# Context tile first in the output stage, matmuls of ones in the last gaps of attention, and the waits of the overflow test inside its chunk

## The chip, the cores and the metric

The kernel runs on one core of a Trainium2 chip. The metric is the time on the device in microseconds, the median over several executions. Before the change the median of three runs is 1055.93 us (1055.47 to 1056.59).

The engines are called PE (TensorE, matmuls), DVE (VectorE), ACT (ScalarE), POOL (GpSimd) and SP (SyncE, which here only issues DMAs). One core has 16 DMA engines.

## What is computed

One layer of a backbone with 512 latent tokens and 128 context tokens, in fp32, D = 1024. Both groups go through the same weights; they differ in the vectors of the adaLN modulation (`g1`, `a2`, `b2` below come from them), in attention and in the scans.

```python
def trunk_layer(x, mod, p, lru_h0, ctx_ckv, ctx_kr):
    sh1, sc1, g1, sh2, sc2, g2 = mod
    h = rmsnorm(x, p['norm1_g']) * (1 + sc1) + sh1
    mix, ctx_state = token_mixing(h, p, lru_h0, ctx_ckv, ctx_kr)
    x = x + g1 * mix
    h = rmsnorm(x, p['norm2_g']) * (1 + sc2) + sh2
    x = x + g2 * hier_moe(h, p)
    return x, ctx_state

# token_mixing ends with
#   o = blocked_attend(q, k, v)                    8 heads
#   gates = sigmoid(h @ w_gate)                    4 branches
#   out = sum(gates * branches) @ w_out

def hier_moe(h, p):
    t = h.reshape(B * L, D)
    g_sel = argmax(t @ w_gr + b_gr)                # 1 of 4 groups
    top_v, top_i = top_k(e_logit of g_sel, 2)      # 2 of its 8 experts
    y = sum over experts of (silu(t @ w1) * (t @ w3) * combine) @ w2   # 32 experts, width 256
```

## The kernel before

It is one program written by hand, engine by engine, with semaphores. Nothing schedules it: the order of each engine's instructions is the order in which the lines of its section stand, and a wait holds all that stands behind it on that engine. The sections are SP (lines 586 to 776), PE (780 to 1409), ACT (1413 to 1711), DVE (1715 to 2429) and POOL (2433 to 2674).

The 640 tokens are `TT` = 5 tiles of 128; tiles 0 to 3 are the latent ones (`LT` = 4) and tile 4 is the context. The stages, by the times of the profiled execution, are:

- **Projections and mixers**, 0 to 270 us. At its start PE runs matmuls of `ones` by `ones` (`spin`, L825) while it waits for weights.
- **Attention**, 270 to 368 us, in 40 units (`UNITS`), each a head and a tile of queries. PE does `scores(i + 2)` and then `probabilities_T(i)` (L1050), which transposes what ACT and DVE made of the scores of unit i. Once in ten units there are the values matmuls (`values`, L1061). The last units are of the context tile, which has one block of keys, so they are short: 5 transposes for a latent unit and one for a context unit.
- **Gates and merge**, 368 to 686.7 us: `h @ w_gate`, the branch products, sums.
- **Output stage**, 686.7 to 790 us. For each tile t and half h of 512 columns: `output(t, h)` (PE, L1172, 8 matmuls with `w_out`, two rows each in the trace), `residual(t, h)` (DVE, L2181 to L2184: times `g1_row`, plus x, times `a2_row`), `x1_T(t, h)` (PE, transposes), sums of squares on ACT, `variance(t)` and `modulated(t)` (DVE: scale and `b2_row`, giving `h2[t]`, which SP stores together with x1), `logits(t, h)` (PE, L1193, 4 matmuls each), `select(t)`, `weights(t)`, `places(t)` and `first(t)` (DVE, the choice of experts and the slot of every token), `counts_ahead`, `prefix` and `table` (PE, small matmuls on it). After the last tile PE runs `first_rows` (L1219, 16 rows for each tile), from which the table of tokens for every expert slot comes; GpSimd gathers rows of h2 by that table (L2615).
- **Experts**, 790 to 1050 us, in 17 units (`UNITS_E`, u = 0 to `LAST` = 16), two experts each but for one. The weights of an expert, 3 MB, go through a ring of six buffers `wexp`, parts of r_a, r_c, r_w, r_ys, r_bv and r_h; SP loads the next w1/w3 (`load_w13`) when `hidden` of the unit in the buffer is done (`s_A`), the next w2 (`load_w2`) when `project` is done (`s_Y`). PE: `pair_T` (L1309), `hidden` (L1316), `hidden_T` (L1323), `project` (L1332). Results are scattered by GpSimd (L2619). An expert has 64 slots; tokens that don't fit go to overflow chunks, and a test between the units 14 and 15 reads their number `n_x` into a register of each engine. With these inputs it is 1, which means that no chunk is run.

The rows `g1_row`, `a2_row` and `b2_row` hold one set for all tiles in the output stage, each 1024 values on 128 partitions. They stand for the latent tiles first and are loaded anew, from `rows_scratch`, for tile 4:

```python
            load_row("xres", g1_row, 0)
            load("xres", x1, x_dram)
            load_row("xres", a2_row, 2)
            load_row("xres", b2_row, 4)
...
                if t == LT - 1:
                    sp.wait_ge(s_x1, 2 * LT)
                    load_row("xres", g1_row, 1)
                sp.wait_ge(s_h2, t + 1)
                if t == LT - 1:
                    load_row("xres", a2_row, 3)
                    load_row("xres", b2_row, 5)
```

so `g1_row` is asked for when `residual(3, 1)` has read it, a2 and b2 when `modulated(3)` has, and `residual(4, 0)` waits for all three.

## Time and profile before

| | us |
|---|---|
| median of 3 runs | 1055.93 |
| profiled execution, its own time | 1059.88 |
| its span | 1058.0 |

| stretch | length | PE busy | DVE busy | clock of PE | DMA share |
|---|---|---|---|---|---|
| projections, 0 to 270 | 270.0 | 260.58 | 138.25 | 0.99 | 0.41 |
| attention, 270 to 368 | 98.0 | 90.01 | 49.30 | 0.98 | 0.08 |
| gates, 368 to 686.7 | 318.7 | 318.70 | 190.35 | 1.00 | 0.27 |
| output, 686.7 to 790 | 103.3 | 100.13 | 61.56 | 0.97 | 0.55 |
| experts, 790 to 1040 | 250.0 | 215.77 | 69.42 | 0.94 | 1.00 |
| end, 1040 to 1058 | 18.0 | 7.88 | 6.58 | 0.82 | 0.32 |

The clock is the granted clock of TensorE as a share of full speed (2.4 GHz); the lower level, 1.2 GHz, is 0.50. The DMA share is the mean busy share of the 16 DMA engines. Over the whole span PE is busy for 993.1 us (94%), DVE for 515.5, POOL for 264.8 and ACT for 232.9. The rows of a timeline give the start, the busy time of a group of like instructions, and in brackets the idle time before it with what ended it. A matmul in fp32 stands as two rows.

### The profile page before, as it was taken

How to read it: one execution, taken by the hardware profiler on the slowest of the kernel's cores; microseconds unless marked ns; L12 is line 12 of the kernel's file. 1: busy time of each engine (PE TensorE's matmuls, PEld its weight loads, DVE VectorE, ACT ScalarE, POOL GpSimd, SP SyncE). 2: the span in 40 equal slices, each digit the busy share in tenths (PEclk: the TensorE clock that was granted, in tenths of full speed). 3: DMA queues.
4: the chain of work that ended last, by engine and by line, in shares of the span. 5: the costliest groups of instructions: out<-in, count | busy, mean ns of one | idle time of the engine just before them, and what ended most of it. 6: DMA issues, size and time to landing. Idle time of an engine off the chain costs nothing.

```text
span 1058.0 us, 11696 instructions
## 1 busy us (share of the span) xinstructions
PE 993.1 (94%) x4304; PEld 590.0 (56%) x4304; DVE 515.5 (49%) x1016; ACT 232.9 (22%) x464; POOL 264.8 (25%) x268
## 2 busy tenths in 40 slices
PE   8999999999899999999999999999989997878776
PEld 6666666655555477777777777645574332322221
DVE  3378652246645345567677555538573331322222
ACT  3223330134555311111111111112111111101011
POOL 0333310011630233445364334100010211110101
PEclk9999999999999999999999999999989998998998
DMA  9745356000000271221312311263489999999994
GB/s 369 300 139 222 120 194 234 1 6 2 1 1 1 100 288 50 80 70 50 100 50 86 143 60 61 80 258 120 159 291 381 335 405 399 400 427 397 403 410 130
DMA packets 37609, 193.65 MB, mean 183 GB/s; under 512 B 7642, under 2 KB 12442, under 8 KB 27696
## 3 DMA queue, kind: packets, MB, share of 16 engines
q1 hardware_dynamic: 32784, 182.31, 44.6%
q0 software_dynamic: 4624, 10.06, 3.9%
q8 instruction: 35, 0.57, 0.2%
q10 hardware_dynamic: 144, 0.52, 0.1%
q14 instruction: 22, 0.18, 0.0%
HBM read 185.50 MB, written 14.09 MB: 189 GB/s over the span
## 4 chain that ended last, share of the span: by engine, by line
PE 79%; DMA 10%; DVE 5%; issue 3%; ACT 2%; SPq 1%; POOL 1%; POOLq 0%; DVEq 0%; ACTq 0%
PE psum L1096 23%; PE psum L1316 9%; PE psum L857 8%; PE psum L1130 7%; DMA r_bv<-in_w_e 4%; PE psum L1332 4%; PE psum L950 3%; PE psum L1172 3%; PE psum L1034 3%; DMA r_ys<-rows_scratch 2%; PE psum L1050 2%; PE psum L802 2%; DMA r_w<-in_w_ada 2%; PE psum L1061 2%; PE psum L979 2%
## 5 line engine op out<-in xcount | busy, mean ns | idle before, releaser
L1096 PE MATMUL psum<-r_h,r_w 128*128 128x320 f32 x512 | 143.6, 433 | 0.0
L2591 POOL TENSOR_TENSOR r_w<-r_w 128x512 f32<-128x512 f32 x64 | 84.7, 1330 | 223.0 <-PE psum L1096 155.9
L1096 PEld LDWEIGHTS psum<-r_h,r_w 128*128 128x128 f32 x512 | 97.1, 190 | 40.6 <-issue 0.3
L1096 PE MATMUL psum<-r_ys,r_w 128*128 128x320 f32 x384 | 111.2, 432 | 0.0
L1096 PEld LDWEIGHTS psum<-r_ys,r_w 128*128 128x128 f32 x384 | 73.0, 190 | 30.4
L1601 ACT ACTIVATE r_bv<-r_bv 128x320 f32<-128x320 f32 x64 | 30.1, 470 | 238.8 <-DVE r_bv L2128 238.8
L2619 POOL DMA_INDIRECT out_y<-r_bv,tab x17 | 26.8, 1576 | 204.7 <-DVE r_bv L2392 204.7
L1172 PE MATMUL psum<-r_w,r_bv 128*128 128x512 f32 x160 | 72.2, 597 | 0.0
L2137 DVE TENSOR_TENSOR r_t<-psum,r_t 128x320 f32<-128x320 f32 x112 | 52.2, 483 | 9.3 <-PE psum L1130 8.0
L1675 ACT ACTIVATE r_t<-psum 128x256 f32<-128x256 f32 x17 | 6.5, 384 | 185.6 <-PE psum L1316 183.7
L2114 DVE SCALAR_TENSOR_TENSOR r_t<-r_bv,r_t 128x320 f32<-128x320 f32 x48 | 46.7, 974 | 1.2 <-ACT r_bv L1601 1.2
L2128 DVE TENSOR_TENSOR sqbuf<-psum,r_bv 128x320 f32<-128x320 f32 x32 | 15.7, 492 | 64.4 <-PE psum L1096 64.4
L2372 DVE COPY r_t<-psum 128x256 f32<-128x256 f32 x17 | 7.2, 424 | 81.1 <-PE psum L1323 81.1
L1172 PEld LDWEIGHTS psum<-r_w,r_bv 128*128 128x128 f32 x160 | 29.2, 190 | 30.3 <-issue 30.1
L1316 PE MATMUL psum<-r_c,r_ckv 128*64 128x512 f32 x64 | 31.9, 648 | 7.9 <-issue 7.9
L2072 DVE TENSOR_REDUCE tinys<-psum 128x1 f32<-128x640 f32 (+1 forms) x40 | 28.6, 716 | 18.5 <-PE psum L1035 18.3
L1034 PE MATMUL psum<-r_a,r_bv 96*128 96x512 f32 x64 | 34.5, 620 | 2.5 <-ACT r_bv L1540 0.8
L2128 DVE TENSOR_TENSOR r_bv<-psum,r_bv 128x320 f32<-128x320 f32 x32 | 15.7, 491 | 41.8 <-PE psum L1096 41.8
L2123 DVE TENSOR_TENSOR r_bv<-r_bv,r_t 128x320 f32<-128x320 f32 x48 | 35.8, 745 | 0.4
L2365 DVE SCALAR_TENSOR_TENSOR r_t<-r_t,psum 128x256 f32<-128x256 f32 x17 | 7.2, 421 | 57.9 <-ACT r_t L1675 57.9
L2441 POOL TENSOR_TENSOR tinys<-tinys 128x2 f32<-128x2 f32 (+2 forms) x11 | 7.6, 688 | 108.3 <-DVE tinys L2189 107.8
L1316 PE MATMUL psum<-r_w,lruw 128*64 128x512 f32 x48 | 24.5, 660 | 5.5 <-issue 5.5
(460 smaller groups left out, 2003.9 us busy)
## 6 DMA issues: line engine op xcount, KB each, us to landing
r_a<-in_w_ada SPq DMA_DIRECT2D x8, 2048.0 KB, 7.8
r_w<-in_w_gate SPq DMA_DIRECT2D x32, 512.0 KB, 4.5
r_a<-in_w_e SPq DMA_DIRECT2D x6, 2048.0 KB, 31.9
r_c<-in_w_e SPq DMA_DIRECT2D x5, 2048.0 KB, 31.2
r_c<-in_w_e SPq DMA_DIRECT2D x8, 1024.0 KB, 34.4
r_w<-in_w_e SPq DMA_DIRECT2D x4, 2048.0 KB, 34.3
r_ys<-in_w_e SPq DMA_DIRECT2D x4, 2048.0 KB, 36.5
r_bv<-in_w_e SPq DMA_DIRECT2D x4, 2048.0 KB, 36.6
```

Of the source, the lines that this page charges most:

```text
L857: ins = mm(dst, w_n[:, k, :], z_mix0[:, k // 2, k % 2, :] if n == 4 else x[:, k, :], start=(k == 0), stop=(k == HK - 1))
L950: mm(o[:, 0:512], x, w[:, 0:512], start=(k == 0), stop=(k == KD - 1))
L1034: mm(o[:, 0:NLAT], q, kT[0:QK, h, 0:NLAT], start=True, stop=True)
L1096: ins = mm(gate_bank(u, n), w[:, k, :], x[:, k, :], start=(k == 0), stop=(k == HK - 1))
L1130: ins = mm(branch_bank(u, seq), x_w[:, k, :], xs_[k], start=(k == 0), stop=(k == kb - 1))
L1172: ins = mm(out_bank(t, n), merged[:, k, t * P:(t + 1) * P], w[:, (k % 4) * D + n * 512:(k % 4) * D + (n + 1) * 512], start=(k == 0), stop= ...
L1316: ins = mm(psum[lo:lo + C, slot, 0:2 * FE], xT[:, k, :], w[:, k * 2 * FE:(k + 1) * 2 * FE], start=(k == 0), stop=(k == KD - 1))
L1332: ins = mm(psum[lo:lo + C, slot, n * 512:(n + 1) * 512], hid[:, f, :], w[:, n * 512:(n + 1) * 512], start=(f == 0), stop=(f == 1))
L2114: v.scalar_tensor_tensor(out=merged[:, 2 * i + j, part] if b == 0 else bquad[n], in0=gth[:, j, part], scalar=1.0, in1=bquad[n], op0=ALU.ad ...
L2123: v.tensor_tensor(merged[:, 2 * i + j, part], merged[:, 2 * i + j, part], bquad[n], ALU.add) \
L2137: v.tensor_tensor(bsum[:, dst, :], branch_bank(u, seq), bsum[:, more, :], ALU.add).then_inc(s_badd, 1)
L2591: g.tensor_tensor(w_mix[n], x, y, op).then_inc(s_wm, 1)
```

## The change

1. **The order of the tiles in the output stage.** `TILE = (4, 0, 1, 2, 3)`: step t now works on tile `TILE[t]`, so the context tile is the first. `side(t)` says whether step t is the context (1) or latent (0) and picks the logits' weights and the column of `info`; `tokens_of(t)` gives its rows. The context's g1, a2 and b2 are loaded first, together with the context's x alone (512 KB); behind a wait for all four, the 2 MB of the latent x. g1 of the latent tiles is asked for after `residual(0, 1)`, a2 and b2 after `modulated(0)`. DVE waits for them before `residual(1, 0)`, where it waited before `residual(4, 0)`.
2. **The order within the first tiles** on PE, DVE and ACT is rewritten: PE does `output(2, 0)` whole before `x1_T(1, 0)`, DVE does `modulated(0)` and `select(0)` before `residual(1, 0)`, ACT does `router_exps(0)` earlier.
3. **`load_w13(4)`**, 2 MB into r_bv, is issued by SP behind `load_w2(3)`, no longer behind the waits for the stores of h2 and x1 and for the first transpose of the experts.
4. **Matmuls of ones on PE** before the last three `probabilities_T` (four each, after a wait for the probabilities of the unit before) and before the last `values` (two).
5. **The overflow test.** PE's waits for `s_yd` (the sums of the unit before are drained) and `s_xTd` move into the chunk, and its reading of `n_x` moves to unit 2.

```diff
+TILE = (LT,) + tuple(range(LT))
...
-            load_row("xres", g1_row, 0)
-            load("xres", x1, x_dram)
-            load_row("xres", a2_row, 2)
-            load_row("xres", b2_row, 4)
+            load_row("xres", g1_row, 1)
+            load("xres", x1[:, 0:1, :], x_dram[:, LT:TT, :])
+            load_row("xres", a2_row, 3)
+            load_row("xres", b2_row, 5)
+            sp.wait_ge(loaded["xres"], 64)
+            load("xres", x1[:, 1:TT, :], x_dram[:, 0:LT, :])
...
-                if t == LT - 1:
-                    sp.wait_ge(s_x1, 2 * LT)
-                    load_row("xres", g1_row, 1)
+                if t == 0:
+                    sp.wait_ge(s_x1, 2)
+                    load_row("xres", g1_row, 0)
                 sp.wait_ge(s_h2, t + 1)
-                if t == LT - 1:
-                    load_row("xres", a2_row, 3)
-                    load_row("xres", b2_row, 5)
+                if t == 0:
+                    load_row("xres", a2_row, 2)
+                    load_row("xres", b2_row, 4)
...
             load_w2(3)
+            load_w13(4)
...
             sp.wait_ge(s_xT, 1)
-            load_w13(4)
...
+                if i >= len(UNITS) - 3:
+                    pe.wait_ge(s_prob, i)
+                    spin(4, (i - 1) % 2)
                 probabilities_T(i)
+            spin(2, 0)
             values(H // 2 - 1, 0, TT)
...
             pe.wait_ge(s_x1, 1)
-            output(2, 0, (0, 1))
-            logits(1, 0)
-            output(2, 0, (2, 3, 4, 5))
-            x1_T(1, 1)
-            output(2, 0, (6, 7))
+            output(2, 0, range(KD))
+            x1_T(1, 0)
             pe.wait_ge(s_x1, 2)
             output(2, 1, (0, 1))
+            x1_T(1, 1)
+            logits(1, 0)
+            output(2, 1, (2, 3))
             logits(1, 1)
...
+                if u == 2:
+                    pe.wait_ge(s_slot, 1)
+                    n_x = pe.value_load(xinfo[0:1, XCH:XCH + 1], min_val=1, max_val=XCH)
                 if u != LAST - 2:
                     continue
 
-                pe.wait_ge(s_yd, LAST - 1)
-                pe.wait_ge(s_xTd, LAST + 1)
-                pe.wait_ge(s_slot, 1)
-                n_x = pe.value_load(xinfo[0:1, XCH:XCH + 1], min_val=1, max_val=XCH)
-
                 def chunk(x):
+                    pe.wait_ge(s_yd, LAST - 1)
+                    pe.wait_ge(s_xTd, LAST + 1)
...
-                if t == LT and h == 0:
-                    dve.wait_ge(loaded["xres"], 112)
+                if t == 1 and h == 0:
+                    dve.wait_ge(loaded["xres"], 128)
...
             residual(0, 0)
             residual(0, 1)
-            residual(1, 0)
             variance(0)
             modulated(0)
+            select(0)
+            residual(1, 0)
+            weights(0)
             residual(1, 1)
-            select(0)
             variance(1)
             modulated(1)
-            weights(0)
```

How this moves instructions, first on PE at the end of attention, before the change (L1050 is `probabilities_T`, L1037 `scores` of a context unit, L1061 `values`):

```order
L1050 MATMUL psum<-consts,r_t 128x128 x5
L1037 MATMUL psum<-r_a,r_bv 128x128
L1050 MATMUL psum<-consts,sqbuf 128x128 x5
L1050 MATMUL psum<-consts,r_d 128x128
L1050 MATMUL psum<-consts,r_t 128x128
L1061 MATMUL psum<-r_c,r_bv 64x512 x10
```

and after it, where the same lines are numbered 1060, 1047 and 1071 and L835 is `spin`:

```order
L1060 MATMUL psum<-consts,r_t 128x128 x5
L1047 MATMUL psum<-r_a,r_bv 128x128
L835 MATMUL psum<-ones 128x128 x4
L1060 MATMUL psum<-consts,sqbuf 128x128 x5
L835 MATMUL psum<-ones 128x128 x4
L1060 MATMUL psum<-consts,r_d 128x128
L835 MATMUL psum<-ones 128x128 x4
L1060 MATMUL psum<-consts,r_t 128x128
L835 MATMUL psum<-ones 128x128 x2
L1071 MATMUL psum<-r_c,r_bv 64x512 x10
```

Each of the last three `probabilities_T` and the values now have matmuls of ones ahead of them.

On SP in the output stage, before the change: `rows_scratch` holds the rows, r_h<-in_x is the load of x, r_ys, r_h, r_w and r_bv<-in_w_e are expert weights, h_scratch and out_y the stores of a tile.

```order
L697 DMA r_w<-in_w_out 128x4096 x2
L588 DMA r_ys<-rows_scratch 128x1024
L588 DMA r_h<-in_x 128x5x1024
L588 DMA r_ys<-rows_scratch 128x1024 x2
L670 DMA r_ys<-in_w_e 128x1024
L721 DMA h_scratch<-r_bv 128x1024
```

and after:

```order
L705 DMA r_w<-in_w_out 128x4096 x2
L596 DMA r_ys<-rows_scratch 128x1024
L596 DMA r_h<-in_x 128x1024
L596 DMA r_ys<-rows_scratch 128x1024 x2
L596 DMA r_h<-in_x 128x4x1024
L678 DMA r_ys<-in_w_e 128x1024
L596 DMA r_ys<-rows_scratch 128x1024 x3
L731 DMA h_scratch<-r_bv 128x1024
```

The x3 of the second set of rows stood ahead of the store of tile 3, and stands now ahead of the first store.

On PE in the expert stage, after the change, behind `project` of unit 2 (L1344); L1403 is the reading of `n_x`, which stood, as L1395, behind `project` of unit 14:

```order
L1344 MATMUL psum<-r_bv,r_t 64x512
L1344 MATMUL psum<-r_ys,r_t 64x512
L1403 TENSOR_LOAD xinfo
L1403 ISA x2
L1328 MATMUL psum<-r_w,r_ckv 64x512
```

The reading now stands ahead of the next unit's `hidden` (L1328) early in the stage.

## Rows read from the trace of the kernel before

**Rows 1.** PE timeline, output stage: start, us, instruction [idle before <-releaser].
```profile
686.66 20.76 PE L1172 MATMUL psum<-r_w,r_bv 128*128 128x512 f32 x48
...
758.72 3.60 PE L1172 MATMUL psum<-r_w,r_bv 128*128 128x512 f32 x8
...
763.18 0.39 PE L1204 MATMUL psum<-r_bv,consts 128*128 128x32 f32 x2
...
767.89 1.95 PE L1172 MATMUL psum<-r_w,r_bv 128*128 128x512 f32 x4
771.94 1.08 PE L1193 MATMUL psum<-w_r,r_t 128*128 128x36 f32 x8 [2.09 <-ACT r_t L1630]
...
775.01 1.89 PE L1193 MATMUL psum<-w_r,r_t 128*128 128x36 f32 x8 [0.69 <-ACT r_t L1630]
```

**Rows 2.** Windows: length, PE, PEld, DVE, ACT, POOL busy, PEclk, DMA share, GB/s.
```profile
362.50:365.50 3.00, 3.00 (x8) 0.91 (x10) 0.00 (x0) 0.00 (x0) 0.64 (x1) 0.50 0.97 347
769.80:775.00 5.20, 2.22 (x17) 1.83 (x16) 4.68 (x17) 2.09 (x5) 0.00 (x0) 1.00 0.79 268
775.00:782.00 7.00, 6.99 (x33) 6.99 (x34) 6.24 (x28) 0.59 (x3) 2.30 (x2) 0.51 1.02 400
788.00:790.00 2.00, 2.00 (x20) 1.96 (x19) 0.27 (x3) 0.18 (x1) 0.93 (x1) 1.00 0.06 25
810.00:812.00 2.00, 2.00 (x11) 0.56 (x8) 0.00 (x0) 0.01 (x1) 0.00 (x0) 1.00 0.51 209
850.00:900.00 50.00, 44.53 (x197) 16.37 (x199) 12.58 (x23) 10.11 (x15) 7.80 (x6) 0.90 1.02 403
```

**Rows 3.** PE timeline of the last units of attention.
```profile
351.96 2.79 PE L1061 MATMUL psum<-r_w,r_bv 128*64 128x512 f32 x12
...
359.44 0.74 PE L1050 MATMUL psum<-consts,sqbuf 128*128 128x128 f32 x5 [0.74 <-issue]
...
362.42 6.01 PE L1061 MATMUL psum<-r_c,r_bv 128*64 128x512 f32 x20 [0.37 <-ACT r_c L1591]
```

**Rows 4.** PE timeline at the start of the kernel: matmuls of ones.
```profile
17.74 3.39 PE L825 MATMUL psum<-ones 128*128 128x128 f32 x28
```

**Rows 5.** VectorE timeline at the tail of the output stage.
```profile
764.24 0.69 DVE L2181 TENSOR_TENSOR consts<-psum,r_ys 128x512 f32<-128x512 f32 x1 [6.58 <-DMA r_ys<-rows_scratch]
...
767.98 0.25 DVE L2208 SCALAR_TENSOR_TENSOR r_bv<-psum,tinys,scond 128x36 f32<-128x36 f32 x1
...
772.20 0.68 DVE L2181 TENSOR_TENSOR consts<-psum,r_ys 128x512 f32<-128x512 f32 x1
```

**Rows 6.** Chain of waits from the tail to the first rows: start us, us, what.
```profile
778.17 7.28 PE psum L1219 x48
...
787.84 1.85 PE psum L1219 x16
```

**Rows 7.** Tile r_ys at 757.7, second set of rows: from issue to landing.
```profile
DMA to landing us min/median/max: 4.0/5.1/6.1
```

**Rows 8.** PE timeline of the last two units.
```profile
1031.21 1.08 PE L1316 MATMUL psum<-r_c,r_ckv 128*64 128x512 f32 x1 [2.99 <-issue]
...
1044.93 0.61 PE L1332 MATMUL psum<-r_c,r_t 128*64 128x512 f32 x1 [0.71 <-DVE r_t L2372]
```

**Rows 9.** VectorE timeline, last unit.
```profile
1048.93 0.69 DVE L2392 TENSOR_TENSOR r_bv<-psum,sqbuf 128x512 f32<-128x512 f32 x1
```

**Rows 10.** Tile r_w at 1014.0, last w2 piece: from issue to landing.
```profile
DMA to landing us min/median/max: 28.3/28.3/28.3
```

**Rows 11.** Tile r_w at 790.7, gather of unit 1: from issue to landing.
```profile
DMA to landing us min/median/max: 7.5/7.5/7.5
```

**Rows 12.** Tile r_w at 820.9, a later gather: from issue to landing.
```profile
DMA to landing us min/median/max: 14.7/14.7/14.7
```

**Rows 13.** PE timeline, pair_T of unit 1.
```profile
800.74 1.10 PE L1309 MATMUL psum<-consts,r_w 128*128 128x128 f32 x8
```

**Rows 14.** Tile r_ys at 689.4 to 690.1, first set of rows: from issue to landing.
```profile
DMA to landing us min/median/max: 15.2/16.0/16.7
```

More of the change, by code:

```diff
@@ L567, in wait_quad_free, with side, tokens_of @@
                 eng.wait_ge(s_mdone, 4 * (u - 3 * OUT_PAIRS) + n + 1)
+        def side(t):
+            return 1 if TILE[t] == LT else 0
+        def tokens_of(t):
+            return slice(TILE[t] * P, (TILE[t] + 1) * P)
         def gate_bank(u, n):
@@ L1188, in logits @@
                 pe.wait_ge(s_htd, 2 * t + h + 1)
-                pe.wait_ge(s_wr, 1 if t < LT else 2)
+                pe.wait_ge(s_wr, 1 + side(t))
                 if t >= 2:
@@ L1192, in logits @@
                 for k in range(KD // 2):
-                    ins = mm(psum[:, 2, t % 2 * 512:t % 2 * 512 + LOGITS], xT[h][:, k, :], w_rm[t // LT][h][:, k, :],
+                    ins = mm(psum[:, 2, t % 2 * 512:t % 2 * 512 + LOGITS], xT[h][:, k, :], w_rm[side(t)][h][:, k, :],
                              start=(h == 0 and k == 0), stop=(h == 1 and k == KD // 2 - 1))
@@ L1236, in _ @@
             output(1, 1, (4, 5))
-            x1_T(1, 0)
             logits(0, 1)
@@ L1251, in _ @@
             prefix(0)
-            output(2, 1, (2, 3, 4, 5))
+            output(2, 1, (4, 5, 6, 7))
             x1_T(2, 0)
-            output(2, 1, (6, 7))
             pe.wait_ge(s_x1, 5)
@@ L1643, in _ @@
             take_x1T(0, 1)
+            router_exps(0)
             squares(1, 0)
@@ L2238, in weights @@
                 dve.wait_ge(s_ract, 2 * t + 2)
-                w1, w2 = (info[:, i * TT + t, 1 + t // LT:2 + t // LT] for i in range(2))
+                w1, w2 = (info[:, i * TT + t, 1 + side(t):2 + side(t)] for i in range(2))
                 step(v.tensor_scalar(top(5), top(3), 1.0, top(2), ALU.add, ALU.mult))
```

16 lines of the change are left out of this document (8 added, 8 removed).

## The prediction

> **What bounds the kernel now.** The question for each edit is which wait ends last where it stands, so the stages are read one by one. TensorE is the bound up to about 770 us: the PE timeline of the output stage shows groups of output matmuls back to back from 686.66 on [rows 1]. From 770 to 775 it is busy for 2.22 of 5.20 us, and from 775 to 782 it is busy all the time at a granted clock of 0.51, that is at the lower of its two levels [rows 2]. After that the DMA engines are the bound: between 850 and 900 their share is 1.02, with PE busy 44.53 of 50 us [rows 2]. Between the two there are two holes of the DMA engines, 788 to 790 (share 0.06) and 810 to 812 (share 0.51) [rows 2]. Both are transfers that wait for PE to free a buffer: as PE begins the expert units earlier, the whole DMA-bound stage, and with it the end, comes earlier by as much. So a microsecond saved on PE before 790 is worth a microsecond at the end. The reader is to carry three places from this: the last gaps of attention, the tail of the output stage, and the last unit.
>
> **Part A, constants in the last gaps of attention.** PE waits 0.74 us before the row at 359.44 and 0.37 before the values matmuls at 362.42, with two more such gaps between, and afterwards the clock is at 0.50 (362.5 to 365.5) [rows 2, 3]. The 20 values rows take 6.01 us there. At full clock 12 such rows took 2.79, so 20 would take 4.65: the lower level costs 1.36 [rows 3]. The new matmuls on ones cost 3.39/28 = 0.12 a row, two rows for each matmul, thus 0.97 for a group of four [rows 4]. They start when the wait for the probabilities before is over and end after the gap of 0.74, so they lengthen the path a little where the gap is shorter than 0.97: I take 0.35 in sum, between nothing (all of it in idle time) and 1.0 (one whole group too much). The gates stage behind has no idle time of PE, so what is won stays. A = 1.36 - 0.35 = +1.0; ends +1.36 and, if the clock falls all the same, -1.0.
>
> **Part B, context tile first.** Before, residual(4,0) could not start until the second set of rows (g1, a2, b2 of the context) had landed: VectorE waits 6.58 us and starts at 764.24 [rows 5], though its matmuls were done about half-way through the x8 group of 758.72, near 760.6 [rows 1]. The change loads the second set between tiles 0 and 1. What is late next at the tail is not 3.6 us earlier all along:
> - places(2), behind residual(4,0) on VectorE, needs prefix(2), which stands on PE at 763.18 [rows 1]; it began at about 766.4, behind the residual's three instructions of 0.7 us from 764.24 [rows 5], and can come 2.7 earlier.
> - residual(4,1), at 772.20 [rows 5], needs output(4,1), which ends at 767.89 + 1.95 = 769.84 [rows 1]. It comes 2.3 earlier.
> - so logits(4,1), at 775.01 [rows 1], starts near 772.7, and with counts and table behind it first_rows starts 2.3 earlier than 778.17 [rows 6]; that is the floor of this part.
> Then the clock. The wait of 2.09 us before logits(4,0) [rows 1] shrinks to about 0.4, and the gaps that remain up to 774.3, around logits(4,0) and before logits(4,1) (0.69 now [rows 1]), are near 0.9 and 0.8. If that keeps the higher level, the 48 rows of 7.28 us take three times 1.85, as the 16 rows at 787.84 do: 1.73 less [rows 6]; and logits(4,1), 1.89 for 8 rows against 1.08 at 771.94, takes 0.8 less [rows 1, 6], of which 0.7 lies on the path. Sum 2.3 + 0.7 + 1.73 = 4.75.
> At the head, x comes in two loads and DVE does modulated(0) and select(0) before residual(1,0). a2 and b2 of the latent tiles are asked for when modulated(0) has ended (about 712.0) and, landing as late as the context's did, 6.1 us [rows 7], are there at 718.1 to 718.5. residual(1,0) stands behind select(0); select(3) took from 767.98 to 772.20, 4.2 us [rows 5], and as select(0) starts near 715.1 it ends at 719.3. So the rows are hidden with 0.8 us left. PE meanwhile has output(2,0) whole: 5 halves of 16 rows at 20.76/48 = 0.43 [rows 1] are 34.6, with x1_T(0) and logits(0) (about 2.2) from 686.66, so it is busy until 723.5, and residual(1,0)'s three instructions end near 721.5. I take off 0.3 for one stall of logits(2,0), which is now closer behind its vectors. B = +4.45, ends +2.0 and +4.75. The rest of this part (tokens' numbers, the side of each tile, the w13 piece of r_ys behind a wait that is over near 701) is address work and costs nothing while the DMA engines have room; without this room the piece would be the first of its buffer to be late, but it is used only from 790 on.
>
> **Part C, waits of the overflow test.** Before the last unit PE is idle 2.99 us (row at 1031.21) [rows 8]: it waits for the last sums of the unit before and then loads the register. Without both, hidden(16) starts 2.99 earlier at best, at 1028.2, and since the row at 1031.21 and those behind it go at the lower level (1.08 us), project(16) could come still a little more than 3.0 before 1044.93 [rows 8]. What is late next is the last w2 piece: asked for at 1014.0, landing 28.3 us later, at 1042.3 [rows 10]. So project(16) starts at 1042.4, the last two rows of VectorE (the first at 1048.93 [rows 9]) come 2.5 earlier, and the scatter behind them is unchanged. C = +2.5; ends 0 (the register's load alone costs the gap) and +3.0 (a landing as early as the stage allows). The register's load at unit 2 may cost PE up to the same 2.99; there the DMA engines are the bound with PE idle a tenth of the time [rows 2], so I count 0. If that cover were gone it would cost 1 to 3. Early w13(4): its buffer is free earlier than it is used, and the stage behind is set by the buffers that PE frees, so no gain; the cost is the second rival.
>
> **Sum.** 1.0 + 4.45 + 2.5 = 7.95. The profiled execution takes 1059.88, so 1051.9 for one like it; it lies 3.95 above the median of 1055.93. Applied to the median: 1055.93 - 7.95 = 1047.98, I say 1047.9.
>
> **The rivals.**
> - The clock falls again at the tail of the output stage. Gaps of 0.4, 0.9 and 0.8 within 4 us stand against the one place where I can read it: at 358 to 362, gaps of 0.4 to 0.8 were enough for 0.50 behind them [rows 2, 3]. Then the 1.73 and the 0.7 are not had: 5.5 in sum, 1050.4. For it: that row. Against it: PE has been at full clock with few gaps for long before. 27%.
>  The Trainium skill, "TensorE: Matmul & The Clock Gate", section "What's actually happening", says that the throttled state is the default and that the share of pulses is set by how busy the array has been recently, not by one wait. By that rule three gaps count in sum, as they did at 358 to 362, and the time would be the 1050.4; only if they count singly is it 1047.9.
> - The gather of unit 1 is late. It took 7.5 us to land when it was issued at 790.7 into the empty DMA engines [rows 11], and a later one 14.7 at 820.9 into full ones [rows 12]. Now w13(4), 2 MB more, stands in the engines ahead of it. Both it and its user, pair_T(1) at 800.74 [rows 13], come 5.45 earlier, at 785.2 and 795.3. With 14.7 it lands at 799.9 and PE waits 4.6: 3.35 in sum, 1052.6. For it: the hole of the DMA engines from 788, through which it went, is filled. Against it: the hole then began near 788 - 5.45 = 782.6, and 2 MB at the 403 GB/s of the row from 850 [rows 2] are 5.2 us, so by 787.8 all is through, 2.6 behind the issue; 7.5 + 2.6 lands at 795.3, just when it is wanted. 12%.
>  The Trainium skill, "DMA: Bandwidth & Descriptors", section "Issuing engines are not separate DMA queues", says that transfers of sync and gpsimd run on the same 16 engines and interleave. By it this is the case; the two landings agree in direction, but whether the queue is full at 785 no row here shows.
> - The ones don't hold the clock, they only delay: A = -0.35, 6.6 in sum, 1049.3. 10%.
> - The waits move and something else stands there (the register's load at unit 2 counts, or the last unit waits for data all the same): C = 0, 5.45, 1050.5. 4%. This is the case in which the change doesn't do what it says.
> - The other side: the second set of rows lands late at its new place. The first set was asked for at 690 while w_out and x were loading, and took 16.7 us [rows 14], against 6.1. The same here is 10.6 late, less the 0.8 in hand: residual(1,0) ends near 731.3 where PE runs dry at 723.5, so it idles 7.4 and 1.7 more at the lower clock. All behind it moves: 9.1 - 7.95 = 1.1 slower, 1057.0. It decides once PE's stall exceeds 8 us, and a little worse landing makes it measurable. Against it: at 712 only w_out's last piece and a 2 MB load ended long before are in the queue. 7%.
>
> **How the numbers follow.** The forecast, 1047.9, has 40%. Its own ends are 1046.8 (A, B and C at their upper ends, 1.36 + 4.75 + 3.0 = 9.1), with 0.6 for the spread of the runs, and 1050. The rivals from 1049.3 to 1052.6 hold 53%. The range is 1046.2 to 1053.0; outside it lie the slow case and combinations of three. A difference under 0.2%, 2.1 us, is what a measurement of this kernel can't tell from no change. All cases but the slow one, and the worst combinations, are faster by more than that: faster 0.87, same 0.06, slower 0.07.
>
> **What would show it.** In the changed kernel's trace: for A, 20 values rows in under 5 us and the clock at 1.00 behind them; for B, no wait of VectorE for rows of its own above 1 us at tile 1 or 4, PE without a gap near 723, the 48 first_rows in 5.6 us, starting near 774.5 (1.0 for A and 2.7 for B before 778.17); the holes of the DMA engines earlier by 5.5 us; for C, no gap of 2.99 before the last unit and project(16) released by the landing of w2. What makes it wrong: PE idle for more than 2 us around 723, the clock at 0.5 behind 775, or pair_T(1) waiting for its gather.

## The result, and the profile after

The changed kernel takes 1053.4 us, the median of 20 runs (1050.22 to 1057.63). The kernel before, measured again beside it, takes 1059.34 over 20 runs (1055.02 to 1063.07). The ratio is 0.9945, with a 95% interval of 0.9932 to 0.9958: 5.8 us faster, 4.4 to 7.2. So the sign was forecast rightly, but the gain of 7.95 lies above the measured interval, and the time lies 0.4 us above the end of the range, 1053.0. Two different things are in that miss. One is the base: the three runs shown had their median at 1055.93, and it is 3.4 us below that of twenty; they are the second to the fourth lowest of the twenty. The other is the gain.

The profiled execution has a span of 1051.3 us against 1058.0, 6.7 less. The stretch behind this is read at three marks on TensorE: the 12 values rows near 351, the start of the output stage, and the first `rowsT` matmuls, with which the expert stage begins. First attention, PE's timeline after the change (L835 the ones, L1060 `probabilities_T`, L1071 `values`), which answers to [rows 3]:

```profile
351.67 2.79 PE L1071 MATMUL psum<-r_w,r_bv 128*64 128x512 f32 x12
...
358.25 1.06 PE L835 MATMUL psum<-ones 128*128 128x128 f32 x8
359.15 0.74 PE L1060 MATMUL psum<-consts,sqbuf 128*128 128x128 f32 x5
359.72 1.06 PE L835 MATMUL psum<-ones 128*128 128x128 f32 x8
...
361.87 0.61 PE L835 MATMUL psum<-ones 128*128 128x128 f32 x4
362.41 4.51 PE L1071 MATMUL psum<-r_c,r_bv 128*64 128x512 f32 x20
```

No idle time is left, and the 20 values rows take 4.51 us where they took 6.01. A group of four costs 1.06, and the values begin 10.74 us behind the 12 rows at 351.67, where it was 10.46 before: the ones delay by 0.28. From the 12 rows to the output stage it is 333.48 us against 334.70, 1.22 less.

Then the tail of the output stage, which answers to [rows 1] and [rows 6] (L1198 `x1_T`, L1207 `logits`, L1233 `first_rows`):

```profile
766.02 1.95 PE L1186 MATMUL psum<-r_w,r_bv 128*128 128x512 f32 x4
767.81 0.98 PE L1207 MATMUL psum<-r_kr,r_t 128*128 128x36 f32 x8
...
769.48 0.66 PE L1198 MATMUL psum<-consts,r_h 128*128 128x128 f32 x4 [0.25 <-DVE r_h L2195]
770.82 1.87 PE L1207 MATMUL psum<-r_krr,r_t 128*128 128x36 f32 x8 [0.69 <-ACT r_t L1642]
...
773.77 3.76 PE L1233 MATMUL psum<-r_ckv,r_bv 128*128 128x128 f32 x16
777.33 2.15 PE L1233 MATMUL psum<-r_ckv,lruw 128*128 128x128 f32 x16
...
781.24 2.03 PE L1233 MATMUL psum<-r_ckv,r_d 128*128 128x128 f32 x16
```

and the windows of the same stretch, with the two places where the DMA engines had their holes (columns as in [rows 2]):

```profile
768.00:770.00 2.00, 1.75 (x16) 1.53 (x14) 1.92 (x3) 0.54 (x2) 0.00 (x0) 1.00 0.51 96
770.00:772.00 2.00, 1.31 (x8) 1.18 (x6) 1.72 (x10) 0.77 (x3) 0.36 (x1) 0.73 0.96 363
772.00:774.00 2.00, 2.00 (x11) 2.00 (x11) 1.93 (x5) 0.00 (x0) 1.94 (x2) 0.50 1.03 401
...
784.00:786.00 2.00, 2.00 (x19) 1.96 (x18) 0.31 (x2) 0.37 (x1) 1.11 (x1) 1.00 1.02 416
806.00:808.00 2.00, 2.00 (x13) 0.62 (x10) 0.00 (x0) 0.20 (x1) 0.00 (x0) 1.00 0.35 141
```

The wait of 2.09 us before logits(4,0) is gone. Idle times of 0.25 and 0.69 are left, and the granted clock still falls, to 0.73 in 770 to 772 and 0.50 behind it: logits(4,1) takes 1.87 and the first 16 rows of `first_rows` 3.76, as in the kernel before. The first 48 rows, from 773.77 to the row at 781.24, take 7.47 us; in the kernel before, the same count from 777.99 takes 7.44. Against the last output matmuls (766.02 and 767.89), logits(4,1), at 770.82 and 775.01, comes 4.19 - 1.87 = 2.32 earlier. That is the floor of part B. The stretch from the start of the output stage to the first `rowsT` is 2.68 shorter, 100.43 against 103.11; the other 0.36 lies ahead of the last output matmuls (80.87 us from the start of the stage against 81.23). The hole from 788 to 790 (0.06) is filled (1.02 at 784 to 786). The one that stood at 810 to 812 now stands at 806 to 808 (0.35), 4 us earlier.

At the other end of that stage VectorE's residual(1,0) starts at 717.91 with no idle time before it, and the loads of the second set of rows landed in at most 8.5 us (the view of tile r_ys, 689 to 725):

```profile
DMA to landing us min/median/max: 3.7/5.3/8.5
```

The gathers of units 0 and 1, issued at 784.9 and 786.5, landed in 7.1 to 7.6 us (tile r_w, 785 to 790), though the DMA engines were full, as the window of 784 shows; [rows 11] had 7.5, issued just behind a window with a share of 0.06:

```profile
DMA to landing us min/median/max: 7.1/7.3/7.6
```

The gathers of the units after them took longer in the same execution: 9.3 us for the one issued at 798.4, 13.5 at 816.7, 17.3 at 828.6 (tile h_scratch).

The end, PE's timeline (L1344 `project`) and the chain of waits (start us, us, what):

```profile
1038.30 0.61 PE L1344 MATMUL psum<-r_c,r_t 128*64 128x512 f32 x1 [1.29 <-DMA r_w<-in_w_e]
```
```profile
1008.02 30.19 DMA r_w<-in_w_e
...
1038.30 3.67 PE psum L1344 x16
...
1042.05 0.69 DVE r_bv L2405
```

The gap of 2.99 before the last unit [rows 8] is gone, and project(16) is released by the landing of the last w2 piece, 30.19 us after its issue, at 1038.21.

### The profile page after: what moved, and what is told of

Its sections match the earlier page's. It is cut to its first block, busy times and chain, and to the rows that moved or that the text cites. A ratio compares the mean times of both kernels' runs of the same rounds, so it can differ in the third digit from the quotient of the medians.

```text
span 1051.3 us, 11753 instructions
## 1 busy us (share of the span) xinstructions
PE 992.0 (94%) x4332; PEld 590.7 (56%) x4332; DVE 516.0 (49%) x1018; ACT 232.9 (22%) x464; POOL 265.0 (25%) x268
## 4 chain that ended last, share of the span: by engine, by line
PE 79%; DMA 10%; SPq 3%; DVE 2%; issue 2%; ACT 2%; POOL 0%; POOLq 0%; DVEq 0%; ACTq 0%
PE psum L1110 23%; PE psum L867 8%; PE psum L1144 7%; PE psum L1186 7%; PE psum L1328 6%; DMA r_bv<-in_w_e 4%; PE psum L960 3%; PE psum L1344 3%; DMA r_w<-in_w_e 3%; PE psum L1044 3%; SPq L678 2%; PE psum L1060 2%; PE psum L812 2%; DMA r_w<-in_w_ada 2%; PE psum L1071 2%
## 5 line engine op out<-in xcount | busy, mean ns | idle before, releaser
L1613 ACT ACTIVATE r_bv<-r_bv 128x320 f32<-128x320 f32 x64 | 30.1, 470 | 238.8 <-DVE r_bv L2141 238.8
L1328 PE MATMUL psum<-r_c,r_ckv 128*64 128x512 f32 x64 | 30.3, 620 | 4.9 <-issue 4.9
L2395 DVE SCALAR_TENSOR_TENSOR sqbuf<-r_d,tab,sqbuf 128x512 f32<-128x512 f32 x17 | 12.8, 751 | 35.0 <-ACT r_d L1706 35.0
```

Source lines behind the costliest of these rows:

```text
L1328: ins = mm(psum[lo:lo + C, slot, 0:2 * FE], xT[:, k, :], w[:, k * 2 * FE:(k + 1) * 2 * FE], start=(k == 0), stop=(k == KD - 1))
```

## The experiments

All were timed beside the kernel before. As executions of one program lie 7 to 11 us apart (and one of the kernel before, beside e3, e5, e7 and e8, took 1249.57), the interval of a ratio is 1.4 to 3 us wide to either side, so the text goes by the stretches of the profiled executions as well. Each row has one profiled execution, and where it says "mean" below, it is a mean over such rows. They are put together here (us; "12 values rows" is their start, the last stretch ends with the last instruction of the chain of waits):

| kernel | 12 values rows | to output stage | to first rowsT | to the end | ratio, 95% interval |
|---|---|---|---|---|---|
| before | 351.96 | 334.70 | 103.11 | 262.80 | 1 |
| changed | 351.67 | 333.48 | 100.43 | 260.10 | 0.9945 (0.9932 to 0.9958) |
| e7 changed, again | 349.06 | 333.49 | 99.55 | 261.98 | 0.9923 (0.9894 to 0.9951) |
| e1 without the ones | 348.86 | 335.16 | 100.55 | 261.64 | 0.9947 (0.9925 to 0.9968) |
| e2 waits back | 350.56 | 333.48 | 99.56 | 263.31 | 0.9944 (0.9927 to 0.9961) |
| e8 the same again | 350.27 | 333.48 | 99.56 | 263.23 | 0.9954 (0.9930 to 0.9979) |
| e3 w13(4) back | 350.68 | 333.48 | 99.58 | 260.24 | 0.9951 (0.9927 to 0.9975) |
| e5 reading of the count back | 354.76 | 333.48 | 101.01 | 260.65 | 0.9951 (0.9932 to 0.9969) |
| e6 before, with ones and waits moved | 352.16 | 333.48 | 103.94 | 261.80 | 0.9982 (0.9965 to 0.9998) |
| e4 ones in the tail | 348.99 | 333.49 | 98.26 | 260.01 | 0.9919 (0.9898 to 0.9939) |
| e9 ones at the front | 349.05 | 333.73 | 99.61 | 262.73 | 0.9940 (0.9916 to 0.9965) |
| e10 front and tail | 349.26 | 333.48 | 98.26 | 262.88 | 0.9933 (0.9907 to 0.9959) |
| e12 ones before project(15) | 350.46 | 333.49 | 99.56 | 260.85 | 0.9928 (0.9904 to 0.9952) |
| e11 all of them | 349.18 | 333.49 | 98.34 | 261.06 | 0.9903 (0.9875 to 0.9931) |

### Without the ones in attention

```diff
-                if i >= len(UNITS) - 3:
-                    pe.wait_ge(s_prob, i)
-                    spin(4, (i - 1) % 2)
                 probabilities_T(i)
-            spin(2, 0)
             values(H // 2 - 1, 0, TT)
```

> The changed kernel without the matmuls of ones in attention. Theory (the ones hold the clock and are worth what the trace of the changed kernel shows, 1.2 to 1.5 us): the values matmuls behind the last probabilities go at half clock again and take about 6.0 us instead of 4.5, the output stage starts 1.2 to 1.5 us later than in the changed kernel, and the gain on the kernel before falls from 5.8 to about 4.5 us (ratio near 0.9957). Rival (the ones only delay, the clock would have been held in this run anyway): values in 4.5 us, output stage not later, ratio 0.9945 or lower.

```profile
356.34 0.74 PE L1060 MATMUL psum<-consts,sqbuf 128*128 128x128 f32 x5 [0.74 <-issue]
357.92 0.30 PE L1060 MATMUL psum<-consts,r_d 128*128 128x128 f32 x1 [0.84 <-issue]
...
359.32 6.21 PE L1071 MATMUL psum<-r_c,r_bv 128*64 128x512 f32 x20 [0.37 <-ACT r_c L1599]
```

The idle times are back and the values rows take 6.21 us. The stretch is 335.16 us against 333.48, and 333.48 is the same to 0.02 in all the kernels with ones but one (333.73). The theory holds at the stretch: the ones are worth 1.2 to 1.7 us. The ratio alone, 0.9947, couldn't have told it from nothing.

### The waits of the overflow test back

```diff
-                if u == 2:
-                    pe.wait_ge(s_slot, 1)
-                    n_x = pe.value_load(xinfo[0:1, XCH:XCH + 1], min_val=1, max_val=XCH)
                 if u != LAST - 2:
                     continue
+                pe.wait_ge(s_yd, LAST - 1)
+                pe.wait_ge(s_xTd, LAST + 1)
+                pe.wait_ge(s_slot, 1)
+                n_x = pe.value_load(xinfo[0:1, XCH:XCH + 1], min_val=1, max_val=XCH)
                 def chunk(x):
-                    pe.wait_ge(s_yd, LAST - 1)
-                    pe.wait_ge(s_xTd, LAST + 1)
```

> The changed kernel with TensorE's waits of the overflow test and the reading of the count back between units 14 and 15. Theory (this part is worth 2.5 us, bounded by the landing of the last w2): an idle time near 3 us before the last unit's first matmuls, project of the last unit released by VectorE as before and not by the DMA, the end about 2.5 us later, ratio near 0.9968. Rival (the DMA engines set the end anyway, so that the waits cost nothing): ratio 0.9945, and project of the last unit still released by the w2 landing.

> The changed kernel once more, beside the runs of this call, because the time of a run scatters by some 3 us and the profiled stretches less. Theory (its gain is A 1.2 to 1.7, order of tiles 2.3 to 2.7, last unit 2.5): 333.5 us from the values matmuls near 351 to the output stage, 100.4 from there to the first rowsT matmuls, 260.1 from there to the end, ratio near 0.9945. Rival (the last unit's part was luck of one profile): 261.6 to 262.8 from the first rowsT matmuls to the end.

> The kernel with the waits and the reading back between units 14 and 15, once more. Theory (they cost 2.5 to 3.2 us at the end): from the first rowsT matmuls to the end 262.6 to 263.3 us, ratio near 0.997. Rival (they cost nothing on average, as the time of the first such run says): the stretch is as long as in the changed kernel beside it, ratio near 0.9945.

```profile
1025.48 0.97 PE L1328 MATMUL psum<-r_c,r_ckv 128*64 128x512 f32 x1 [2.95 <-issue]
...
1039.29 0.61 PE L1344 MATMUL psum<-r_c,r_t 128*64 128x512 f32 x1 [0.71 <-DVE r_t L2385]
```

The gap of 2.95 is back, and project(16) is released by VectorE again. The last stretch is 263.31 and 263.23 (262.80 in the kernel before) against 260.0 to 262.9 in the nine profiles, of other kernels too, in which TensorE doesn't wait there and no ones stand before project(15). Their mean is 261.3, that of the three 263.1. So the part is worth 1.8 us by these profiles and between 0 and 3 in one execution. The times don't show it: the interval of e2, 0.9944, excludes the 0.9968 that was expected, that of e8, 0.9954, holds both 0.997 and 0.9945. The theory of e7, 260.1 each time, fell with its own profile of 261.98: there are two lengths of this stretch, which the last experiments take up.

### Only the reading of the count back

```diff
-                if u == 2:
-                    pe.wait_ge(s_slot, 1)
-                    n_x = pe.value_load(xinfo[0:1, XCH:XCH + 1], min_val=1, max_val=XCH)
                 if u != LAST - 2:
                     continue
+                pe.wait_ge(s_slot, 1)
+                n_x = pe.value_load(xinfo[0:1, XCH:XCH + 1], min_val=1, max_val=XCH)
                 def chunk(x):
```

> The changed kernel with only the reading of the count back between units 14 and 15; the waits for VectorE's sums stay in the chunk. Theory (the wait for the sums is the larger part, 1.6 of 3.0 us, and the reading the rest, 1.4): an idle time of 1.3 to 1.6 us before the last unit's first matmuls, little of it on the path because the last w2 lands later, end 0 to 0.5 us later than the changed kernel. Rival (the reading of a register is the whole cost): idle time of 3 us there and the same end as with all waits back.

PE at the place of the reading, the last row of project(14) and the first of hidden(16):

```profile
1027.80 0.59 PE L1344 MATMUL psum<-r_bv,r_t 128*64 128x512 f32 x1
1028.23 0.59 PE L1328 MATMUL psum<-r_c,r_ckv 128*64 128x512 f32 x1
```

Both the theory and the rival fell: there is no idle time at all. Where no wait stands ahead of it, reading the register doesn't hold up the matmuls. The view of the line with the reading shows why (e5):

```profile
L1405 PEldq TENSOR_LOAD <-xinfo x1: 485/485/485, 1024.8 to 1024.8; - x1
```

The reading ran at 1024.8 to 1025.5, 3.4 us before the first row of hidden(16), when project(14) had just begun. In the kernel before it stood behind the waits, as the same view and the chain of waits (start us, us, what) show:

```profile
L1395 PEldq TENSOR_LOAD <-xinfo x1: 481/481/481, 1029.8 to 1029.8; - x1
```
```profile
1028.50 1.30 DVE r_bv L2392 x2
1029.80 1.42 issue
```

So of the gap of 2.99 us there, some 1.6 are the wait for VectorE's sums, and 1.4 the reading (1029.8 to 1030.6) with what follows it. The theory had divided the gap rightly; what fell is that the reading would cost its part without the wait too. No run has the waits back without the reading, so what the waits alone cost isn't measured.

### The w13 load back

```diff
             load_w2(3)
-            load_w13(4)
...
             sp.wait_ge(s_xT, 1)
+            load_w13(4)
             load_w2(4)
```

> The changed kernel with the load of w13(4) back behind the waits for the stores and the first transpose of the experts. Theory (the early load fills the hole of the DMA engines before the expert stage but opens another behind, since TensorE frees the buffers, so it is worth nothing): the DMA share falls to near 0.1 for 2 us just before the first rowsT matmuls, the dip of 794 to 798 (0.80) goes, the time from the first rowsT matmul to the end is the same within 1 us, ratio near 0.9945. Rival (it is worth its 2 MB, 5 us of DMA time): end 3 to 5 us later, ratio near 0.998.

The last stretch is 260.24, among the shortest. The hole is smaller than expected (share 0.78 for 2 us at 782 to 784, before the first rowsT at 783.74), and the dip behind it is gone, as expected. So 2 MB issued some 9 us earlier bring nothing that this shows, and the rival's 3 to 5 us are out. The explanation that was expected, that TensorE sets when the ring frees its next buffer, fits both dips, but no run tests it by itself.

### The kernel before, with ones in attention and the waits moved

Its diff is the parts 4 and 5 of the change.

> The kernel before with the matmuls of ones in attention and with the waits of the overflow test moved (reading of the count at unit 2), but with the old order of tiles and the old place of the w13 load. Theory (the order of tiles is worth 2.3 us and the parts add up): VectorE still waits 6 to 7 us for the rows before residual(4,0), the gain is 1.3 + 2.5 = 3.8 us less noise, ratio near 0.9964. Rival (the order of tiles brought nothing or the parts overlap): ratio near 0.9945.

VectorE waits for the second set of rows as before:

```profile
763.22 0.69 DVE L2185 TENSOR_TENSOR consts<-psum,r_ys 128x512 f32<-128x512 f32 x1 [6.54 <-DMA r_ys<-rows_scratch]
```

Attention is at its 333.48, and the stretch to the first rowsT is 103.94, against 99.55 to 101.01 in the nine profiles of the new order without ones in the tail (mean 99.9). With the 103.11 of the kernel before, mean 103.5, the order of tiles is worth 3.6 us on average. The time, 1.9 us faster (0.2 to 3.7), is less than the 3.8 expected: the last stretch gave 1.0, not 2.5. Against the kernel before alone the order of tiles is worth 3.2 us; e6 takes 0.8 longer there than the kernel before, as its clock fell earlier and logits(4,0) took 1.70 us instead of 1.08.

### Ones in the tail of the output stage

```diff
             logits(4, 0)
             counts_ahead(3)
             prefix(3)
+            spin(1, 2)
             x1_T(4, 1)
+            spin(3, 2)
             logits(4, 1)
```

> The changed kernel with one matmul of ones before x1_T(4,1) and three before logits(4,1), where TensorE is idle for 0.25 and 0.69 us in the trace of the changed kernel before its clock falls to the lower level. Theory (the idle time in sum drops the clock there, and that is the 2.4 us missing from the prediction): the clock stays at 1.00 from 770 to 778, the 48 rows of first_rows take 5.6 us instead of 7.3, the expert stage begins 2.0 to 2.4 us earlier, ratio near 0.9925. Rival (it falls because of the many short matmuls with few columns, so that filling the gaps is not enough): the clock is still 0.50 behind 771, and the kernel is 0 to 0.3 us slower than the changed one.

```profile
766.40 0.47 PE L835 MATMUL psum<-ones 128*128 128x128 f32 x2
766.82 0.65 PE L1198 MATMUL psum<-consts,r_h 128*128 128x128 f32 x4
767.31 0.83 PE L835 MATMUL psum<-ones 128*128 128x128 f32 x6
768.16 1.08 PE L1207 MATMUL psum<-r_krr,r_t 128*128 128x36 f32 x8
769.79 0.65 PE L1223 MATMUL psum<-r_t,sqbuf 128*128 128x48 f32 x4 [0.55 <-DVE sqbuf L2266]
...
770.48 2.03 PE L1233 MATMUL psum<-r_ckv,r_bv 128*128 128x128 f32 x16
772.35 1.95 PE L1233 MATMUL psum<-r_ckv,lruw 128*128 128x128 f32 x16
```
```profile
768.00:770.00 2.00, 1.44 (x12) 1.18 (x10) 1.83 (x8) 0.11 (x1) 1.03 (x2) 1.00 1.04 399
770.00:772.00 2.00, 2.00 (x19) 2.00 (x19) 1.86 (x7) 0.30 (x2) 1.27 (x1) 1.00 1.00 401
772.00:778.00 6.00, 6.00 (x56) 6.00 (x54) 5.21 (x25) 0.29 (x1) 0.00 (x0) 1.00 1.02 363
```

Only 0.94 us of idle time was filled. The granted clock stays at 1.00, though a wait of 0.55 us for VectorE is still there, and the first 16 rows take 2.03 instead of 3.76. The stretch is 98.26 us, 2.2 shorter than in the changed kernel's first profile and 1.3 to 2.8 shorter than in all nine. This is most of the clock's 2.43 us that the forecast counted and the change doesn't get, shown by supplying it; e10 and e11, which have the same ones, repeat it with 98.26 and 98.34, and the ratio, 0.9919, points the same way. The first 48 rows take 5.58 to 5.59 us in these three profiles and 7.2 to 8.1 in all nine of the new order without the ones; the kernel before had 7.4. In six of the nine (e2, e3, e7, e8, e9, e12) logits(4,1) does go at full clock, 1.08 us, and `first_rows` starts 7.1 us after the start of the last output matmuls instead of 7.7, but the clock falls behind the next wait of 0.55.

### Ones at the front

The 12 values rows begin anywhere from 348.86 to 354.76 us, in kernels that don't differ up to there. Here are two executions at the end of a wait for the adaLN weights (PE, of the kernel before and of e4):

```profile
23.28 2.85 PE L802 MATMUL psum<-r_w,scond 128*32 128x512 f32 x16 [2.15 <-DMA r_w<-in_w_ada]
26.92 1.94 PE L813 MATMUL psum<-consts,r_bv 128*128 128x128 f32 x8 [0.79 <-ACT r_bv L1431]
```
```profile
23.46 1.92 PE L812 MATMUL psum<-r_w,scond 128*32 128x512 f32 x16 [2.27 <-DMA r_w<-in_w_ada]
26.20 1.06 PE L823 MATMUL psum<-consts,r_bv 128*128 128x128 f32 x8 [0.81 <-ACT r_bv L1445]
```

The clock fell after a wait of 2.15 us in one and not after 2.27 in the other; by 32 us this costs 2.8 us. Of the eleven profiles without ones here it fell behind this wait in four (kernel before, changed, e5 and e6, waits of 1.95 to 2.38) and not in six (e1, e2, e4, e7, e8, e12, waits of 1.92 to 2.39); in e3 the rows start at 24.29 with no wait, behind a lower clock (0.78 from 20 to 24). In e5 a second fall, at the start of attention, adds about as much. Windows around the second scores:

```profile
270.00:276.00 6.00, 5.26 (x23) 3.25 (x22) 3.14 (x5) 2.18 (x4) 2.40 (x5) 1.00 0.00 0
276.00:282.00 6.00, 5.15 (x16) 3.41 (x15) 3.33 (x6) 4.29 (x7) 0.42 (x1) 0.57 0.00 0
```

In e2, e8 and e12 a shorter fall at the same place (0.83 to 0.85 from 276 to 282) puts the values rows at 350.3 to 350.6 where e1, e4 and e7, without any fall, have 348.9 to 349.1.

```diff
-            spin(14, 3)
+            spin(22, 3)
...
             for i in range(2):
+                if i:
+                    spin(3, 3)
                 scores(i)
```

> The changed kernel with 22 matmuls of ones instead of 14 before the wait for the adaLN weights that ends at 23.3 us, and three before the second scores at 277 us. Theory (the 3 us by which executions of one kernel differ before 350 us come from the clock, which after the same idle times, 2.05 to 2.3 us at 23.3 and 0.75 and 0.85 at 275 to 277, falls in one execution and not in another): the weight matmuls at 23.3 take 1.92 us and not 2.85, the 12 values rows begin at 349.0 or up to 0.3 later, never at 351 to 355, and the median falls by 1 to 2 us against the changed kernel, ratio near 0.993. Rival (the scatter is of the transfers): the values rows begin anywhere from 349 to 355 and the ratio stays 0.9945.

> The changed kernel with matmuls of ones at all three places: before 23.3 us, before the second scores, and in the tail of the output stage (one before x1_T(4,1), three before logits(4,1)). Theory (each place is held, and they add up): values rows at 349.0, 98.3 us from the output stage to the first rowsT matmuls, span 1046 to 1048, ratio near 0.991, the fastest of all. Rival (a gain ahead of the expert stage is given back in the DMA-bound stage): the stretch from the first rowsT matmuls to the end grows by more than 1 us beyond the 260.0 to 262.0 of the changed kernel.

They begin the values rows at 349.05 and 349.26, e11 below at 349.18, with the rows near 23.46 in 1.92 us: three of three without a fall, against three of the eleven profiles without these ones. The seven runs of e9 lie within 3.5 us (1051.54 to 1055.07), but those of e10 within 5.4 (1048.54 to 1053.98), so that the times scatter less isn't shown. The medians fall less than expected, to 0.9940 and 0.9933, and the last stretch is long, 262.73 and 262.88. That of e10 is 0.9 us beyond the upper end of 262.0, just short of the 1 us that its rival named. That what was won ahead is partly given back at the end is thus possible, but not shown: e4, which won as much in the tail, has 260.01.

### Ones before project(15)

```diff
+                if u == LAST - 1:
+                    pe.wait_ge(s_yd, u)
+                    spin(9, Y_SLOT[u])
                 for i in AT[u]:
                     pe.wait_ge(w2_loaded[i % NBUF], 16 * pieces_until(W2_PIECES, i))
```

In the changed kernel's second profile the end is no longer a matter of transfers alone (PE):

```profile
1023.87 0.64 PE L1328 MATMUL psum<-r_c,r_ckv 128*64 128x512 f32 x1 [0.53 <-DMA r_w<-in_w_e]
...
1030.11 1.09 PE L1344 MATMUL psum<-r_h,r_t 128*64 128x512 f32 x1 [2.59 <-issue]
...
1030.99 1.06 PE L1344 MATMUL psum<-r_h,r_t 128*64 128x512 f32 x1
```

PE waits 2.59 us for the w2 of unit 15, whose load (tile r_a) was issued at 1000.0 and landed 30.1 us later; the clock falls, and project(15) runs its first rows at 1.06 to 1.09 us instead of 0.59, on the path: project(16), at 1036.46, is released by VectorE and not by its w2.

> The kernel with ones at all three places, and nine more matmuls of ones before the wait for w2 ahead of project of unit 15. Theory (the two lengths of the last stretch, 260.0 to 260.7 and 261.6 to 262.9, differ because TensorE's clock falls in the wait of 2.6 us before project(15) in the longer ones, so that project(15) goes at 1.2 GHz on the path): no fall of the clock behind 225 us of the expert stage, 260.0 to 260.8 from the first rowsT matmuls to the end, span near 1047, ratio near 0.990. Rival (the two lengths come from when the last transfers land): 261.6 to 262.9 still, project(16) later by what the ones delay.

> The changed kernel with only the nine matmuls of ones before the wait for w2 ahead of project of unit 15. Theory (as for the kernel above, the fall of the clock there): 260.0 to 260.8 from the first rowsT matmuls to the end, whichever way the clock went before; ratio 0.5 us under that of the changed kernel, 0.994. Rival (ones delay project(15) where TensorE would not have waited): 261 to 262.

```profile
1027.09 2.27 PE L835 MATMUL psum<-ones 128*128 128x128 f32 x18
1029.72 0.61 PE L1348 MATMUL psum<-r_h,r_t 128*64 128x512 f32 x1 [0.35 <-issue]
...
1034.62 0.61 PE L1348 MATMUL psum<-r_c,r_t 128*64 128x512 f32 x1 [0.88 <-DMA r_w<-in_w_e]
```

In e11 the wait is filled but for 0.35 us, all rows are at 0.59 to 0.64, and project(16) is released by the DMA again. The stretch is 261.06: 1.7 to 1.8 less than in e9 and e10, but 0.3 more than the theory's upper end, and not in the rival's 261.6 to 262.9 either. The traces show two causes of the two lengths, the clock and the landing of the w2 of unit 15 (tile r_a; us behind the first `rowsT`, as for the stretch):

| kernel | w2 of unit 15 lands | longest row of project(15) | to the end |
|---|---|---|---|
| changed | 246.5 | 0.59 | 260.10 |
| e5 | 247.7 | 0.64 | 260.65 |
| e1 | 247.5 | 1.06 | 261.64 |
| e7 | 248.0 | 1.11 | 261.98 |
| e10 | 248.8 | 1.12 | 262.88 |
| e11 | 248.7 | 0.64 | 261.06 |

In e1, e7 and e10, with the lower clock, the end comes 14.0 to 14.1 us behind the landing, wherever that lies. e11 lands as late as e10 and ends 1.8 earlier: that is the clock. So of the 2.8 us between the first profile and e10 the clock is some 1.8, and the later landing the rest. The later landing goes together with something earlier: near 225 us of the stage TensorE waits 3.2 to 3.7 us in the changed kernel, e3, e4, e5 and e12, and its clock falls, while in e1, e6, e7, e9, e10 and e11 it waits 1.6 to 2.1 us and goes on at 0.61 us a row. Which of the two brings the other isn't shown.

In e12 the stretch is 260.85. The w2 landed at 1030.80, and the ones, which began at 1029.79, held project(15) until 1031.99, 1.2 us later; project(16) is released by VectorE. So the ones delayed there, as the rival had it, but the stretch lies between the two forecasts, and e12 decides nothing. With all the ones, e11 takes 1050.14 us (median of 6): 0.9903 of the kernel before, 10.3 us less (7.3 to 13.3), the fastest median here. Its interval, up to 0.9931, just clears the changed kernel's first interval (from 0.9932) but not the second (0.9894 to 0.9951).

## Why the prediction was right or wrong

**The base is the step that failed.** "Applied to the median: 1055.93 - 7.95 = 1047.98" took three runs as the kernel's time. The profile page had 1059.88 for its own execution, "3.95 above the median", and the sum was moved down by that difference. But the profiled execution was the typical one: the median of 20 is 1059.34. This alone puts the time outside the range: 1055.93 less the measured gain of 5.8 is 1050.1, inside it. Why three runs taken together all lay so low is open. Part of the scatter of 8 us could have been suspected from the trace of before, where 16 weight rows take 2.85 us at 23.28 and 1.92 at 15.88. The range gave "0.6 for the spread of the runs". With the sum against the profiled execution, 1051.9, and 2 to 3 us for this, it would have held 1053.4.

**Part A** was put at +1.0 and measured 1.22 in the first pair of profiles, up to 1.7 against e1. Values rows at full clock were worked out as 4.65 and took 4.51; the delay of the ones, taken as 0.35, was 0.28. The rival that they only delay is out.

**Part B** was put at +4.45, of which 2.3 was called the floor and 2.43 hung on the clock. The floor came to 2.32 us. **The step of the gain that failed is the clock's 2.43**: 1.73 of it, the 48 rows of `first_rows` at full clock, was had in none of the nine profiles of the new order (7.2 to 8.1 us, where the forecast had 5.6), and the 0.7 of logits(4,1) in six of them. So the first rival came true, with a gain worked out as 5.5 us, where the measured one is 5.8. That these agree so well is partly luck, as C came out smaller too. What decided was the weighing of the idle times near logits(4,1): less than a microsecond of them (0.25 and 0.69 in the first profile) stood ahead of the fall, and e4, which fills them, has no fall. The row at 358 to 362 had said so ([rows 2, 3]) and was given 27%; the rule of the Trainium skill, "TensorE: Matmul & The Clock Gate", section "What's actually happening", that recent activity as a whole sets the clock, pointed the same way, and e4 agrees with it: with ones in both idle times, 1.00 stays instead of 0.50. On average over the profiles B is 3.6 us (3.2 against the kernel before alone), as the fall comes sooner in some executions and later in others (the first 16 rows take 2.88 to 3.76). At the head, where the forecast took off 0.3 for a stall, 0.36 was gained. That the parts of the head are hidden held: no wait for rows, PE without a gap near 723. The other side, rows that land 16.7 us late, was 8.5 at most.

**Part C** was put at +2.5, by the landing of the last w2. The mechanism held in the first profile, 2.7 us. It isn't the whole: in five of the nine profiles with the waits moved (e1, e6, e7, e9, e10) the w2 of unit 15 lands later and the clock falls in the wait for it, which costs some 1.8 us (e11 against e10), and the average gain is 1.8. The prediction looked only for the transfer that lands last and not for TensorE's level behind the new wait, which its own part B teaches. That reading the register at unit 2 costs nothing was right, and e5 shows that it would have cost nothing at the old place either, once the waits ahead of it were gone.

**The early w13** was put at nothing and is worth nothing (e3). **The gather** as a rival didn't come true: 7.1 to 7.6 us through full DMA engines, and pair_T(1), at 796.55, has no wait. Its price, the 14.7 us of a later gather at 820.9 [rows 12], is no odd value: from the fourth on, the gathers of the changed kernel take 10.5 to 17.3 us. What makes the first two fast at the same share, 1.02, is open. "DMA: Bandwidth & Descriptors" of the Trainium skill, section "Issuing engines are not separate DMA queues", says that they interleave, and that agrees with the 7.6 us at a share of 1.02; taking it to mean that the gather waits behind the 2 MB was the error here.

**The sum** of the profiles is 1.2 + 3.6 + 1.8 = 6.6 us, inside the measured 4.4 to 7.2. Of the 1.35 missing from the forecast 7.95, B is 0.85 and C 0.7, while A gave 0.2 more. The term most mis-sized is thus the clock's: 2.43 forecast, none had in the first pair, and in the other profiles at most the 0.6 of logits(4,1) and 0.2 in the 48 rows; the rest of the 3.6 is the head and the clock that e6 lost.

## What to carry to other kernels

Where the granted clock falls behind idle times, as TensorE's does here, price a removed wait twice: the time of the wait and the level behind it, and look whether the idle times that remain, in sum, stand ahead of another fall; four matmuls of constants in them brought here 1.7 us on average on top of the 3.6 of the reordering. Before a sum is set against a median, compare the profiled execution with the runs: a difference larger than the spread shown is scatter that the range must hold. And when gains are smaller than the scatter of a run, judge the parts by stretches between fixed marks, with more than one profile of each: from the values rows to the output stage they agreed here within 0.02 us where the times differed by 3, but the stretch at the end scattered by 2.9 us and had to be taken apart first.

## What the runs showed of the hardware

- The same wait drops TensorE's clock in one execution and not in another: at one place of the program, waits of 1.95 to 2.38 us did in four profiles and waits of 1.92 to 2.39 didn't in six. It costs 2.8 us there, and at a second place 1.5 us or, in e5, 2.8; the two make most of the 5.9 us between the earliest and the latest start of the values rows.
- Behind idle times of 0.25 and 0.69 us the granted clock fell to 0.50 (in six of nine profiles only behind a third, of 0.55); with ones in the first two, and the third left, it stayed at 1.00 in all three profiles.
- Reading a register from memory on TensorE, with no wait ahead of it, left no gap between the matmuls around it (1027.80 to 1028.23, the spacing of 0.43 of the rows before): it ran 3.4 us ahead of the matmul behind it. Behind a wait it stood in the gap, with 0.8 of the 3.0 us.
- A gather issued from GpSimd with the DMA engines at a share of 1.02 landed in 7.6 us, later ones in such a stage in 10.5 to 17.3 us, while loads issued from SyncE there took 28 to 30 us.
